# Decoder step with product-key experts: a quarter of the dense expert projections computed in the map stage, five gather places, one raw U buffer

## What is computed

```python
e = i1 * N_KEYS + i2
g = jax.nn.softmax(cv, axis=-1)
a = jax.nn.gelu(jnp.einsum('td,thkd->thk', tb, u_tab[e]).astype(jnp.float32), approximate=False)
return jnp.einsum('thk,thkd->td', (g * a).astype(tb.dtype), v_tab[e])
```

## Time and profile before

| | us |
|---|---|
| median of 3 runs | 3907.29 (3895.41 to 3909.98) |
| the profiled execution, timed | 3909.41 |
| its span in the profile | 3907.8 |
| map stage, first group's matmul to the last | 1534.8 to 1887.1 |
| expert loop, TensorE | 1903.1 to 3821.4 |
| TensorE, DVE, GpSimd, ScalarE busy, share of the span | 84, 68, 41, 35% |
| DMA moved, mean | 991 MB, 254 GB/s |

### The profile page before, as it was taken

How to read it: one execution, slowest core, us unless ns; L and a number is a source line. 1 busy time by engine, 2 the same in 40 slices (tenths; PEclk the granted TensorE clock), 3 DMA queues, 4 the chain that set the end, 5 groups by cost and what they waited for, 6 DMA issues and landing times. The chain is left out here.

```text
span 3907.8 us, 58722 instructions
## 1 busy us (share of the span) xinstructions
PE 3267.4 (84%) x20561; PEld 2846.2 (73%) x20561; DVE 2644.8 (68%) x5883; ACT 1348.8 (35%) x3194; POOL 1591.6 (41%) x1343
## 2 busy tenths in 40 slices
PE   6999788566687975656699999999999999999994
PEld 3676455211277964555599999999999999999993
DVE  4224776110234799989688888888888888888885
ACT  3010566000221113879433323333323333333331
POOL 0010000000212444999645545545546455455450
PEclk8999899777788987888899999999999999999997
DMA  6632873999412122665688888888888888888883
GB/s 226 239 131 73 236 215 114 367 414 410 165 65 89 60 76 71 251 245 204 273 311 332 314 311 340 321 320 339 306 327 322 317 335 316 315 336 312 320 293 136
DMA packets 280369, 991.41 MB, mean 254 GB/s; under 512 B 21925, under 2 KB 139536, under 8 KB 215865
## 3 DMA queue, kind: packets, MB, share of 16 engines
q1 hardware_dynamic: 214648, 480.71, 34.0%
q0 software_dynamic: 62784, 469.88, 31.8%
q10 hardware_dynamic: 2752, 38.75, 2.6%
HBM read 909.52 MB, written 146.80 MB: 270 GB/s over the span
## 5 line engine op out<-in xcount | busy, mean ns | idle before, releaser
L2210 PE MATMUL e_pa<-k_hi_d,e_uh 128*128 128x320 f32 x2048 | 616.0, 314 | 77.7 <-DVE e_act L2371 62.1
L2211 PE MATMUL e_pa<-k_lo_d,e_uh 128*128 128x320 f32 x2048 | 605.5, 309 | 0.0
L2410 POOL DMA_INDIRECT e_uv<-peer_uv,k_g_idx x416 | 400.6, 963 | 498.2 <-DVE e_pY L2351 442.5
L2339 DVE CUSTOM_DVE_ANT_0 e_uv<-e_uv,e_h 128x1024 f32<-128x1024 f32 x416 | 504.2, 1212 | 61.3 <-DMA e_uv<-peer_uv,k_g_idx 60.6
L2351 DVE SCALAR_TENSOR_TENSOR e_pY<-e_uv,e_wts,e_pY 128x1024 f32<-128x1024 f32 x412 | 527.3, 1280 | 0.0
L2210 PEld LDWEIGHTS e_pa<-k_hi_d,e_uh 128*128 128x128 f32 x2048 | 385.5, 188 | 103.6 <-DVE e_act L2371 87.7
L2405 POOL TENSOR_TENSOR e_vl<-e_v,e_vh 128x1024 fp32r<-128x1024 f32 x128 | 308.9, 2413 | 294.5 <-ACT e_vh L2262 294.0
L2289 ACT ACTIVATE e_gel<-e_dots 128x1 f32<-128x1 f32 x416 | 83.4, 200 | 956.2 <-DVE e_dots L2339 953.4
L2232 PE MATMUL e_po<-e_ph,e_vh 128*128 128x320 f32 x2048 | 387.4, 311 | 16.8 <-DVE k_OT L2385 12.3
L2211 PEld LDWEIGHTS e_pa<-k_lo_d,e_uh 128*128 128x128 f32 x2048 | 385.7, 188 | 0.0
L2241 PE MATMUL e_po<-e_pl,e_vh 128*128 128x320 f32 x2048 | 384.0, 309 | 0.4
(11 more groups left out here) (332 smaller groups left out, 5868.9 us busy)
## 6 DMA issues: line engine op xcount, KB each, us to landing
k_kv<-kv_pages SPq DMA_DIRECT2D x128, 512.0 KB, 6.7
s_kv<-kv_state SPq DMA_DIRECT2D x32, 2048.0 KB, 17.3
e_v<-peer_uv SPq DMA_DIRECT2D x128, 512.0 KB
e_u<-peer_ut SPq DMA_DIRECT2D x126, 512.0 KB
s_g<-r_G SPq DMA_DIRECT2D x10, 4096.0 KB
k_OT<-s_g SPq DMA_DIRECT2D x64, 640.0 KB
v_win_sample<-state_v_win POOLq DMA_DIRECT2D x28, 1168.0 KB
k_win_sample<-state_k_win ACTq DMA_DIRECT2D x28, 1168.0 KB
```

The source lines that it names most:

```text
L2210: nc.tensor.matmul(pa[:, m % 2, 0:WD], uh[:, c % 2, k], keep.hi_d[:, k, cols], start=(k == 0), stop=False)
L2211: nc.tensor.matmul(pa[:, m % 2, 0:WD], uh[:, c % 2, k], keep.lo_d[:, k, cols], start=False, stop=False)
L2339: nc.vector.tensor_tensor_reduce(uv[:, r, 0:D], uv[:, r, 0:D], h[:], 1.0, 0.0, ALU.mult, ALU.add, dots[:, r:r + 1]).then_inc(row_dotted, 1)
L2410: nc.gpsimd.indirect_dma_start(uv[:, s % RING], None, io["peer_uv"], bass.IndirectOffsetOnAxis(ap=keep.g_idx[:, s:s + 1], axis=0),).then_i ...
```

## The change

**In the map stage.** The projections of the first chunk of each of the 32 iterations (`EARLY` = 32 chunks, `HALVES` = 64 halves) are computed there. `made_by` spreads their 64 x 24 matmuls evenly behind the groups 11 to 159; `half_at(n)` is the group behind which half n is complete. The U chunks are loaded by SyncE into two buffers in memory that the queries have left (`uu`), split by ScalarE (`split_u`) and GpSimd (`low_u`) into the buffers of the query weights, and the finished halves go through PSUM places of the score stage and `pout` to a new DRAM array `s_p` (`dots_away`, `store_p`; 32 x 320 KB). Since those PSUM places held transposed picks, DVE copies these away once (`keep_turned`). The loads of late score tiles (`load(n)`) stand at fixed groups in SyncE's order now, no longer one per tile.

**In the expert loop.** `dot` runs for the chunks 1 to 3. `gelus` and `weigh` of m = 0, 1 take `early`, which SyncE loads from `s_p`, in place of `pa`. The low part `pl` is made by GpSimd (`low_p`), and DVE waits for it two halves later. U has one raw buffer in place of two; `RING` is 5; `hrow` and `grow` share memory. The V splits stand beside the halves 1, 2, 4, 5 (before 0, 2, 4, 5), the U splits beside half 3 and the outputs 0 and 6 (before halves 1, 3 and outputs 0, 2), and the row steps are dealt out anew.

```diff
+        EARLY = NQ
+        OPENS = 3 * SLOTS
+        HALVES = NBD * EARLY
+        PER_HALF = 3 * KC
...
+        def made_by(done):
+
+            return max(0, HALVES * PER_HALF * (done + 1 - OPENS) // (ND * NGT - OPENS))
...
+                def load_u(e):
+                    if e >= 2:
+                        sp.wait_ge(ul_done, e - 1)
+                    sp.dma_start(uu[:, e % 2], io["peer_ut"][CQ * e]).then_inc(u_in[e % 2], 16)
...
-                for i in range(ND):
-                    if i + 1 < LATE:
-                        load(i + 1)
-                    store(i)
...
+                for done in range(ND * NGT):
+                    for n in range(1, LATE):
+                        if done == rows_before(SPOTS * (n - 1)) + OPENS:
+                            load(n)
+                    for e in range(EARLY):
+                        if e >= 2 and done == (half_at(NBD * (e - 4) + 1) + SLOTS + 1 if e >= 4 else 2 * SLOTS + e):
+                            load_u(e)
+                        if done == half_at(NBD * e + 1) + 2:
+                            store_p(e)
+                    if done % GROUPS == GROUPS - 1:
+                        store(done // NGT, done % NGT // GROUPS)
...
+                        for n in range(HALVES):
+                            if NGT * i + g == half_at(n) + 1:
+                                dots_away(n)
+                                if n % NBD == NBD - 1 and n // NBD + 2 < EARLY:
+                                    split_u(n // NBD + 2)
...
+                            for e in range(2, EARLY):
+                                if done + u == half_at(NBD * (e - 2) + 1) + SLOTS:
+                                    low_u(e)
...
+                        for m in range(made_by(done - 1), made_by(done)):
+                            early_dot(m)
...
-RING = 4
+RING = 5
...
-        uu = sb("e_u", [P, 2, KC, P])
+        uu = sb("e_u", [P, KC, P])
...
-        grow = sb("e_grow", [P, D])[:]
+        grow = hrow
...
-        V_AT = (0, 2, 4, 5)
+        V_AT = (1, 2, 4, 5)
...
-        BESIDE = (2, 2, 2, 1, 2, 1, 1, 0) + (0,) + (1,) * (OUTS - 1)
+        BESIDE = (1, 2, 2, 2, 2, 2, 1, 0) + 2 * ((0,) + (1,) * (OUTS // 2 - 1))
...
-                    for c in range(CQ):
-                        dot(i, c)
-                    out(i)
+                with pe.Fori(0, NQ // 2) as j:
+                    for half in range(2):
+                        for c in range(1, CQ):
+                            dot(2 * j + half, half, c)
+                        out(2 * j + half)
...
+                    if n >= 2:
+                        v.wait_ge(pl_done, n - 1)
...
-                    gathers(i, ops[:1])
-                    v.wait_ge(ph_done, n + 1)
-                    nc.vector.tensor_tensor(pl[:, c, cols], act_out[:, m % 2], ph[:, c, cols], ALU.subtract).then_inc(pl_done, 1)
-                    gathers(i, ops[1:])
+                    gathers(i, share(m))
...
+                def low_p(i, m):
+                    n, c, b = DOTS * i + m, m // NBD, m % NBD
+                    cols = slice(b * WD, (b + 1) * WD)
+                    pool.wait_ge(ph_done, n + 1)
+                    nc.gpsimd.tensor_tensor(pl[:, c, cols], act_out[:, m % 2], ph[:, c, cols], ALU.subtract).then_inc(pl_done, 1)
...
+                        if m == 3:
+                            low_u(UQ * i + 2)
                         if m in V_AT:
                             low_v(CQ * i + V_AT.index(m))
+                        low_p(i, m)
                         gathers(i, m)
```

More of the change, by code:

```diff
@@ L1652, in width, with half_at @@
             return P if i < NT else TS
+        def made_by(done):
+            return max(0, HALVES * PER_HALF * (done + 1 - OPENS) // (ND * NGT - OPENS))
+        def half_at(n):
+            return next(g for g in range(ND * NGT) if made_by(g) >= PER_HALF * (n + 1))
         with nc.Block() as block:
@@ L2367, in weigh @@
                     cols = slice(b * WD, (b + 1) * WD)
-                    ops = share(m)
+                    own = early[:, b * WD:(b + 1) * WD] if c == 0 else pa[:, m % 2, 0:WD]
+                    if n >= 2:
+                        v.wait_ge(pl_done, n - 1)
                     v.wait_ge(g_in[c // 2], 16 * i + 16)
```

184 lines of the change are left out of this document (142 added, 42 removed).

## The result

The changed kernel takes **4006.97 us** (median of 4 runs, 4000.77 to 4011.35), the kernel before beside it 3907.01 (4 runs, 3895.41 to 3909.98): ratio **1.026**, 95% interval 1.0235 to 1.0286. It is 100 us slower, where 27 us faster was forecast, and outside the range.

The account below looks back on a forecast made before the run. TensorE's work was taken to bound the expert loop; -118 us there and +91 us in the map stage, against the median of 3907 us, gave 3880 us, range 3800 to 3950 us.

Parts of the forecast that it names:

- the chain on GpSimd: Expert loop: splits, low parts and gathers before the first output take 22.4 us, from t = 6.5 to 28.9.
- TensorE's stand at the first output: Expert loop: sign that TensorE stands some 5 us an iteration for GpSimd's low part.
- the G store's hole: Map stage: ScalarE's 10.7 us stand for the G store goes, with loads put at fixed groups.
- the map stage's engines: Map stage: TensorE's pace 418 us, plus 18 us where GpSimd waits for DVE, against 353 before.
- Rival B: Expert loop: DMA takes over, gathers 2 us late give 57.8 us an iteration, -54 us, 3946 us in all; 13%.
- Rival A: Expert loop: GpSimd's chain isn't late, TensorE sets an iteration of 52 us, 3760 us in all; 12%.
- With the 184 matmuls left (26.9 us) the iteration ends at t = 55.8.: Expert loop: after the wait, an iteration of 55.8 us saves 3.7 us, 32 times: -118 us.
- TensorE sets the pace.: Map stage: 2.65 us a group with early matmuls, against 2.5 for GpSimd and 2.4 for ScalarE: 418 us.
- And the U loads: +8 us.: Map stage: U loads queued behind 4 MB stores, at 18 us a store, cost 8 us.
- rival C: Map stage: U loads late behind stores, ScalarE waits more than 20 us in all; +138 us, 3929 in all; 18%.
- One raw U buffer: ... covered by those 10 us: Expert loop: next U load issued at about t = 17.6, wanted at t = 28, so no cost.
- The forecast's own case: Whole kernel: the forecast's own mechanisms, with the sums' small errors, give 3840 to 3920 us; 57%.

Follow-up runs that it names:

- e1: The changed kernel with the low parts of the activations back on DVE: 3824.4 us, ratio 0.978.
- e2: The changed kernel with 23 extra matmuls, results unused, filling TensorE's waits at each iteration's first output: 3962.0 us, ratio 1.014.
- e7: e4 with seven of the 24 matmuls of each early half left out: 3958.8 us, ratio 1.014.
- e11: The changed kernel with activation and map-stage U low parts on DVE, stores in pieces, early-store wait and load moved, K copies issued with query blocks: 3795.1 us.
- e12: e11 with the map stage's low parts of U left on GpSimd instead of DVE: 3820.6 us, ratio 0.978.
- e4: The changed kernel with the map stage's 28 K window copies cut to 64 elements a sequence: 3964.9 us, ratio 1.015.
- e13: e11 with 16 of the window copies at the dense tokens' query blocks and 12 in the stage mix_out: 3750.1 us, ratio 0.962.
- e5: The changed kernel with each 4 MB store cut into four 1 MB pieces, one group apart: 3994.2 us, ratio 1.023.

## Why the prediction was wrong

Right as stated: the chain on GpSimd and its times (t = 6.7, 8.1 and 29.3 against 6.5, 7.9 and 28.9), the 0.88 us of a low part inside its bounds, TensorE's stand at the first output (4.1 us; "some 5 us", though as one wait for a low part, where the trace has three, the longest for a V split), the G store's hole gone, the map stage's engines (352 to 428 without transfers' waits, +76, against 418 + 18 - 353 = +83). Rival B did not happen: DVE waits 9.6 us in 1000 for gathers after the change, and e1 runs with DMA at 0.95 at a shorter iteration. Rival A was wrong as a forecast of this kernel; e1 shows the 52 us that it named, once the chain is gone.

Wrong, with the sizes:

1. *"With the 184 matmuls left (26.9 us) the iteration ends at t = 55.8."* They take 28.6 us, since the clock is at half behind the wait. That, and a chain 0.4 us later, make 58.0: 1.6 us gained by the loop's mean in place of 3.7, -49 us in place of -118. The term was mis-sized by 69 us; e2 gives 45 of them back, and the rest wasn't divided. No row of before stood behind 26.9 us after a wait of 4 us: the longest wait there was 1.7 us.
2. *"TensorE sets the pace."* It did not: GpSimd does (e7, and e11 against e12), at 428 us without the waits for transfers (e4). That this lies close to the 436 forecast is luck. Only with both other causes gone is TensorE the fullest engine (e13).
3. *"And the U loads: +8 us."* The waits for transfers cost 45 us (e4 against after). This is rival C's mechanism in part (27.3 us of waits for U; its bound was "more than 20 us in all"), and an equal part that the forecast did not have at all: the stores of early halves, which free `pout`, stand in the same queue behind the same 4 MB. Those 4 MB pieces are 19 us of it (e5); with the window copies away both waits vanish. Together with point 2 this makes 121 in place of 91.
4. The seam, +23 us, had no term. The last early store and a load from it stand on the way into the loop, and the change's text shows both. And *"One raw U buffer: ... covered by those 10 us"* was worked out for an iteration and not for the start, where SyncE waits 14.9 us for U's splits with the map's loads behind it.

The sum: -49 + 121 + 23 + 5 = +100, where -118 + 91 = -27 was put. The forecast's own case was given 57% and a slower kernel 24%; no rival held the clock behind the wait, the stores of early halves or the seam.

The Trainium skill, page DMA: Bandwidth & Descriptors, section "Queues, rings and completion order", has each DMA engine go round the queue rows that have work, a packet at a time. By that rule copies in ScalarE's row take a share from whatever SyncE's row wants, though no transfer of theirs stands ahead of it. e4, e11, e12 and e13 agree: 45 us (e4), 44 (e11 and e13) and 29 (e12) of the map stage go with copies that no engine waits for. A share of the queue can't be told from other reasons there.

Open: whether a shorter wait at the first output would leave the clock alone, and how much of the seam's other 16 us two raw U buffers would give back, was not tried.

## What to carry to other kernels

Price a wait that a change puts into TensorE's stream twice: its length, and what the matmuls behind it cost at half the clock; here 4.1 us of waits cost 5.7. Work moved off an engine with room to one that feeds the bound engine can cost more than the work removed: take each part of a change alone (here dropping one of its parts turned +100 us into -79). And copies that nobody waits for belong where no small transfer that someone waits for runs beside them; look at the DMA share and at who waits, since a stage at 0.57 can still stand for its transfers.
